# A down projection as seven half-size products per pair of chunks, with its sums on GpSimd and VectorE

## The chip, the cores and the metric

The kernel runs on one core of a Trainium2 chip. The metric is the time of one execution on the device in microseconds (us). Engines are named as in the profile: PE is TensorE, DVE VectorE, ACT ScalarE, POOL GpSimd, SP SyncE, which issues the transfers.

## What is computed

One layer of a decoder for a prompt of 2048 tokens and 32 sample tokens, width 1024. The change concerns the last product of the layer, from the gated activations (2816 wide) to the model width, its residual and the final norm:

```python
h2 = rms_norm(x, p['norm2_w']) * (1.0 + sc2) + sh2
u, val = jnp.split(h2 @ p['w_up'], [D_FF], axis=-1)
u, fbuf_new = causal_dwconv(u, fbuf, p['ffconv_w'], p['ffconv_b'])
x = x + g2 * ((jax.nn.silu(u) * val) @ p['w_down'])
...
y = rms_norm(x, final_w)
```

Inputs and outputs are float32.

## The kernel before

A float32 product is made of float16 parts: each operand is scaled by a power of two and cut into a high part (ScalarE, `ACT.Copy` with a scale) and a low part (VectorE, value times scale minus the high part). `three_passes` (L343) issues three matmuls for one product: high by high, high by low, low by high.

The layer runs in phases, one block of engine programs each; a phase starts when all engines have ended the one before. Inside a phase each engine works through its own program in the order in which it is written, and semaphores order the engines among themselves. The last two phases matter here.

`phase_up` walks over 22 blocks of 128 hidden columns, in three groups of tokens each. It makes its product in seven half-size products as well (`UpWeights`, L2177, whose four weight sums run on GpSimd), writes the activations to DRAM (`act_cols`, one row of 128 hidden columns per block) and keeps their maxima, from which the scale of the next product follows. It also reads `w_down` tile by tile for the weights' maximum. At its end SyncE loads the first two weight pieces and the first part of chunk 0 (`core.first_raw`, `core.first_a`).

`phase_down` (L2694) has the 16 prompt chunks of 128 tokens and one chunk of 32 sample tokens. For a chunk, `product` runs over 22 tiles of K and two halves of the 1024 output columns, 22 x 2 x 3 = 132 matmuls of 128x128 by 128x512, into two PSUM banks; the other two banks serve the next chunk. During chunk 0 the weights arrive in 11 pieces of 2048 columns; ScalarE cuts their high parts (L2819), VectorE their low parts (L2876), and they stay in SBUF as `d_w`. For each chunk ScalarE and VectorE cut the activations in one instruction each (L2812, L2853, 2816 columns). `finish` on VectorE scales the product by the gate (L2863), adds the residual (L2866), waits for ScalarE's sum of squares (L2824), forms the mean (L2868), waits for GpSimd's power of -1/2 (L2908), and multiplies by the final norm (L2870). SyncE stores the rows and loads the next.

## Time and profile before

| | us |
|---|---|
| median of 3 runs | 2749.71 (2747.45 to 2750.07) |
| the profiled execution | 2748.17 |
| its span, first to last instruction | 2746.0 |
| TensorE busy in the span | 2503.5 (91%) |
| VectorE, ScalarE, GpSimd busy | 1675.2, 837.0, 401.8 |
| mean granted clock of TensorE | 0.951 of full speed |

Times inside a profile are counted from the first instruction. A matmul's busy time is longer than its pitch, since matmuls overlap in the engine; the pitch is read from starts. Granted clock 1.00 is 2.4 GHz, 0.50 is 1.2 GHz.

### The profile page before, as it was taken

To read this page: it belongs to the slowest core of one execution; us is meant where nothing else is said; L and a number is where in the kernel's file an instruction comes from. 1 tells how busy PE (TensorE), PEld (TensorE's weight loads), DVE (VectorE), ACT (ScalarE), POOL (GpSimd) and SP (SyncE) were. 2 spreads that over 40 slices of the span, in tenths; PEclk is the share of its full clock that TensorE was granted. 3 is DMA by queue.
4 is the path that set the end of the run, shared out by engine and by line. 5 is a ranking of instruction groups with operands and counts; after the bars stand their busy time and mean duration, and the time that the engine had idled before them with its cause. 6 is when DMAs were issued, how large, how long until landed. Compare 5 with 4: busy or idle time off the path is not lost. (4 is left out here: it accounts for less than half of the span.)

```text
span 2746.0 us, 44479 instructions
## 1 busy us (share of the span) xinstructions
PE 2503.5 (91%) x17421; PEld 1544.9 (56%) x17421; DVE 1675.2 (61%) x3344; ACT 837.0 (30%) x1273; POOL 401.8 (15%) x384
## 2 busy tenths in 40 slices
PE   2699999969998999599969999999999979999998
PEld 0355555558766777455446666666666643444444
DVE  6445565546888787578867777777777765222221
ACT  2324343214434444144422222222223233111110
POOL 0123232300000000012232222122211200000000
PEclk6799999979999999699989999999999999999999
DMA  8335433370232311333311222122221236323221
GB/s 257 104 114 166 147 123 126 117 232 29 85 146 96 144 55 54 101 119 119 118 54 59 72 77 73 62 64 72 77 73 57 70 132 195 110 73 99 82 79 41
DMA packets 194618, 279.69 MB, mean 102 GB/s; under 512 B 16296, under 2 KB 131544, under 8 KB 192332
## 3 DMA queue, kind: packets, MB, share of 16 engines
q1 hardware_dynamic: 194517, 278.34, 31.2%
q8 instruction: 63, 1.03, 0.2%
q14 instruction: 38, 0.31, 0.0%
HBM read 203.02 MB, written 75.29 MB: 101 GB/s over the span
## 5 line engine op out<-in xcount | busy, mean ns | idle before, releaser
L345 PE MATMUL d_po<-d_w,w_heads 128*128 128x512 f16 x704 | 269.1, 382 | 17.2 <-DVE d_w L2876 16.5
L346 PE MATMUL d_po<-d_w,w_heads 128*128 128x512 f16 x704 | 268.9, 382 | 0.0
L347 PE MATMUL d_po<-d_w,w_heads 128*128 128x512 f16 x704 | 268.9, 382 | 0.0
L2379 PE MATMUL py<-h_parts,w_heads 128*128 128x384 f16 (+1 forms) x792 | 246.0, 311 | 18.1 <-DVE u_p L2521 18.1
L2380 PE MATMUL py<-h_parts,w_heads 128*128 128x384 f16 (+1 forms) x792 | 245.8, 310 | 0.0
L2381 PE MATMUL py<-h_parts,w_heads 128*128 128x384 f16 (+1 forms) x792 | 245.8, 310 | 0.0
L345 PE MATMUL prj<-w_heads,h_parts_t 128*128 128x512 f16 x512 | 195.8, 382 | 10.8 <-DVE h_parts_t L962 5.4
L2863 DVE SCALAR_TENSOR_TENSOR d_out<-d_po,d_scale,g_p 128x1024 f32<-128x1024 f32 x16 | 20.5, 1284 | 288.6 <-PE d_po L347 288.5
L346 PE MATMUL prj<-w_heads,h_parts_t 128*128 128x512 f16 x512 | 195.6, 382 | 0.0
L347 PE MATMUL prj<-w_heads,h_parts_t 128*128 128x512 f16 x512 | 195.5, 382 | 0.0
L345 PE MATMUL m_prj<-m_h,w_heads 128*128 128x128 f16 (+1 forms) x1088 | 178.8, 217 | 12.9 <-DMA m_h<-h_parts 11.6
L2379 PE MATMUL px<-h_parts,w_heads 128*128 128x384 f16 (+1 forms) x528 | 164.5, 312 | 17.5 <-PEq L1841 17.5
L346 PE MATMUL m_prj<-m_h,w_heads 128*128 128x128 f16 (+1 forms) x1088 | 178.8, 217 | 0.0
L347 PE MATMUL m_prj<-m_h,w_heads 128*128 128x128 f16 (+1 forms) x1088 | 178.7, 217 | 0.0
L2380 PE MATMUL px<-h_parts,w_heads 128*128 128x384 f16 (+1 forms) x528 | 164.5, 311 | 0.0
L2381 PE MATMUL px<-h_parts,w_heads 128*128 128x384 f16 (+1 forms) x528 | 164.5, 311 | 0.0
L2379 PE MATMUL pz<-h_parts,w_heads 128*128 128x384 f16 (+1 forms) x528 | 163.9, 310 | 0.0
L2380 PE MATMUL pz<-h_parts,w_heads 128*128 128x384 f16 (+1 forms) x528 | 163.9, 310 | 0.0
L2381 PE MATMUL pz<-h_parts,w_heads 128*128 128x384 f16 (+1 forms) x528 | 163.9, 310 | 0.0
L2674 POOL TENSOR_TENSOR u_vz<-u_val,u_cv 128x384 f32<-128x384 f32 (+1 forms) x66 | 60.4, 914 | 621.8 <-DVE u_cv L2561 410.1
L2812 ACT ACTIVATE w_heads<-w_heads,mscale 128x2816 f16<-128x2816 f32 (+1 forms) x16 | 40.5, 2532 | 351.2 <-PE d_po L347 340.3
L345 PEld LDWEIGHTS d_po<-d_w,w_heads 128*128 128x128 f16 x704 | 69.3, 98 | 103.1 <-issue 11.9
(471 smaller groups left out, 5652.0 us busy)
## 6 DMA issues: line engine op xcount, KB each, us to landing
C_new<-in_w_up_dram SPq DMA_DIRECT2D x11, 2048.0 KB, 7.5
w_heads<-in_w_up_dram SPq DMA_DIRECT2D x44, 512.0 KB, 5.8
w_heads<-act_cols SPq DMA_DIRECT2D x15, 1408.0 KB, 7.2
act_cols<-w_heads SPq DMA_DIRECT2D x44, 384.0 KB, 2.3
win_raw<-in_w_in_dram SPq DMA_DIRECT2D x8, 2048.0 KB, 13.9
win_raw<-in_w_ada_dram SPq DMA_DIRECT2D x8, 2048.0 KB
first_a<-in_w_down_dram SPq DMA_DIRECT2D x22, 512.0 KB, 3.7
w_heads<-in_w_down_dram SPq DMA_DIRECT2D x11, 1024.0 KB, 6.3
```

The source lines that it names most:

```text
L345: nc.tensor.matmul(out, left[0], right[0], start=(k == 0), stop=False)
L346: nc.tensor.matmul(out, left[0], right[1], start=False, stop=False)
L347: return nc.tensor.matmul(out, left[1], right[0], start=False, stop=last)
L2379: nc.tensor.matmul(out, left[0], right[0], start=(start and k == 0), stop=False, skip_group_check=True)
L2380: nc.tensor.matmul(out, left[0], right[1], start=False, stop=False, skip_group_check=True)
L2381: last = nc.tensor.matmul(out, left[1], right[0], start=False, stop=(k == KC // 2 - 1), skip_group_check=True)
L2674: last = nc.gpsimd.tensor_tensor(of_half(vz, g, 1), by_pair(ov, g), of_half(cv, g, 1), ALU.mult)
L2812: nc.scalar.activation(ap[buf][:, 0, :, 0:T], a[:, :, 0:T], ACT.Copy, scale=a_scale(c)).then_inc(s["a_hi"], 1)
L2863: last = nc.vector.scalar_tensor_tensor(out=out[0:T], in0=of, scalar=ks[0:T, group(c):group(c) + 1], in1=g[0:T], op0=ALU.mult, op1=ALU.mult)
```

## The change

The 16 prompt chunks become eight pairs. K is split into two halves, the output columns into two halves, and a pair has two chunks of tokens: a two-by-two product of blocks, which Strassen's form (Winograd's variant) makes of seven block products, each with a sum of activation blocks and a sum of weight blocks. The 11 steps over K (`J`) are now the outer loop and the seven products the inner one, each with a PSUM bank of its own; a step is 7 x 3 = 21 matmuls of 512 columns. There are 88 steps, `n` from 0 to 87, pair `i` and K step `j`.

- Weights: for each of the 11 steps GpSimd makes four sums of 128x512 (`sums_w`); ScalarE and VectorE cut three own blocks and four sums (1536 and 2048 columns). 11 transfers of 1 MB, in a ring of three buffers. Step 0's are loaded, summed and cut during the last block of `phase_up`.
- Activations: for each step two transfers of 128 KB into a ring of three; GpSimd makes two sums of 128x128 (`sums_13`), VectorE two more (`sums_24`), and both cuts have 896 columns. Two buffers of parts.
- The seven banks are put together into four output blocks by five VectorE additions that read PSUM and two in SBUF; ScalarE copies two banks out (`keep`). Gate, residual, mean and norm of the two chunks are placed behind steps 0 to 5 of the next pair.
- The sample tokens come after the last pair, as four column groups over 11 steps: 132 matmuls of 512 columns.
- The weights' maximum is found two blocks from the end of `phase_up` (`search`), each tile of `w_down` one block earlier.

The core of the diff (the same waits are on the other engines where they are left out):

```diff
+class DownParts:
...
+    J = FB // 2
+    RAW = (0, 0, 1, 2, 0, 1, 2, 0, 1, 2, 1)
+    SUM = (0, 0, 1, 0, 1, 0, 1, 0, 1, 0, 1)
+    W_OF = (0, 2, 1, 6, 3, 4, 5)
+    A_OF = (1, 2, 6, 0, 3, 4, 5)
...
+    def load_w(self, sp, j):
+        p = self.last_user(self.RAW, j)
+        if p is not None:
+            sp.wait_ge(self.w_lo, 2 * p + 1)
+            sp.wait_ge(self.w_summed, p + 1)
+        sp.dma_start(self.raws[self.RAW[j]].rearrange("p (h n) -> p h n", h=2), self.src_w[j]).then_inc(self.w_in[self.RAW[j]], 16)
...
+    def sums_w(self, pool, j):
+        b, t = self.raw(j), self.tsum(j)
+        b12, b11, b22, b21 = (b[:, q] for q in range(4))
+        p = self.last_user(self.SUM, j)
+        self.w_landed(pool, j)
+        if p is not None:
+            pool.wait_ge(self.w_lo, 2 * p + 2)
+        steps = Steps(pool, self.w_steps, 2 * j)
+        self.nc.gpsimd.tensor_tensor(t[:, 2], b22, b12, ALU.subtract)
+        steps.then(self.nc.gpsimd.tensor_tensor(t[:, 0], b12, b11, ALU.subtract))
+        steps.then(self.nc.gpsimd.tensor_tensor(t[:, 1], b22, t[:, 0], ALU.subtract))
+        self.nc.gpsimd.tensor_tensor(t[:, 3], t[:, 1], b21, ALU.subtract).then_inc(self.w_summed, 1)
+    def w_parts(self, j, i):
+        w = self.slot(j)
...
+    def hi_sums(self, act, j):
+        act.wait_ge(self.w_summed, j + 1)
+        to, of = self.w_parts(j, 0)[1]
+        self.nc.scalar.activation(to, of, ACT.Copy, scale=self.core.mscale[:, 1:2]).then_inc(self.w_hi, 1)
+    def lo_part(self, dve, j, q):
+        dve.wait_ge(self.w_hi, 2 * j + q + 1)
+        (lo, of), (hi, _) = self.w_parts(j, 1)[q], self.w_parts(j, 0)[q]
+        self.nc.vector.scalar_tensor_tensor(out=lo, in0=of, scalar=self.core.mscale[:, 1:2], in1=hi, op0=ALU.mult, op1=ALU.subtract).then_inc(self.w_lo, 1)
+    def a_raw(self, n):
...
+    def load_a(self, sp, n):
+        i, j = divmod(n, self.J)
+        if n > 3:
+            sp.wait_ge(self.a_lo, n - 2)
+        raw = self.a_raw(n)[:, 0:4].rearrange("p (c h) t -> p c h t", c=2)
+        src = self.src_a[j][:, :, 2 * i * P:2 * (i + 1) * P].rearrange("p h (c t) -> c p h t", c=2)
+        sem = self.a_in[3 if n == 0 else n % 3]
+        for c in range(2):
...
+    def sums_13(self, pool, n):
+        a = self.a_raw(n)
+        pool.wait_ge(self.a_in[3 if n == 0 else n % 3], 32 if n == 0 else 32 * ((n + 2) // 3))
+        self.nc.gpsimd.tensor_tensor(a[:, 4], a[:, 0], a[:, 1], ALU.add)
+        self.nc.gpsimd.tensor_tensor(a[:, 6], a[:, 2], a[:, 0], ALU.subtract).then_inc(self.a_half, 1)
+    def sums_24(self, dve, n):
+        a = self.a_raw(n)
+        dve.wait_ge(self.a_half, n + 1)
+        self.nc.vector.tensor_tensor(a[:, 5], a[:, 4], a[:, 2], ALU.subtract).then_inc(self.a_steps, 1)
+        dve.wait_ge(self.a_steps, n + 1)
+        self.nc.vector.tensor_tensor(a[:, 7], a[:, 3], a[:, 5], ALU.subtract).then_inc(self.a_summed, 1)
+    def wait_step(self, eng, n):
+        i, j = divmod(n, self.J)
+        if j == self.J - 1:
+            eng.wait_ge(self.prod, 7 * (i + 1))
+        else:
+            eng.wait_ge(self.k_done, (self.J - 1) * i + j + 1)
+    def cut_a_hi(self, act, n):
+        act.wait_ge(self.a_summed, n + 1)
+        if n > 2:
+            self.wait_step(act, n - 2)
+        self.nc.scalar.activation(self.a_parts(n)[:, 0], self.a_raw(n)[:, 1:8], ACT.Copy, scale=self.a_scale(n // self.J)).then_inc(self.a_hi, 1)
+    def cut_a_lo(self, dve, n):
+        dve.wait_ge(self.a_hi, n + 1)
+        to = self.a_parts(n)
+        self.nc.vector.scalar_tensor_tensor(out=to[:, 1], in0=self.a_raw(n)[:, 1:8], scalar=self.a_scale(n // self.J), in1=to[:, 0],
+                                            op0=ALU.mult, op1=ALU.subtract).then_inc(self.a_lo, 1)
...
-            sp.wait_ge(s["p3"], UG * (FB - 1))
-            sp.dma_start(core.first_raw[0], pairs[0]).then_inc(core.first_in[0], 16)
             sp.wait_ge(up.lo_cut, FB)
-            sp.dma_start(core.first_raw[1], pairs[1]).then_inc(core.first_in[1], 16)
+            dn.load_w(sp, 0)
...
+            dn.load_a(sp, 0)
             body(FB - 1, 1, False)
+            dn.load_w(sp, 1)
...
+                        if last:
+                            act.wait_ge(s["p3"], UG * b)
+                            dn.hi_own(act, 0)
+                        else:
+                            up.cut_hi_sums(act, b + 1, 1 - u)
+                    if g == 2 and last:
+                        dn.hi_sums(act, 0)
...
+            dn.cut_a_hi(act, 0)
...
+                    if g == 0 and search:
+                        dve.wait_ge(s["wd_maxed"], FB)
+                        nc.vector.tensor_reduce(tops.red[:, 0:1], wd_max[:], AX.X, ALU.max).then_inc(tops.found, 1)
...
+                    if g == 2:
+                        if last:
+                            dn.sums_24(dve, 0)
+                            dn.lo_part(dve, 0, 0)
+                        else:
...
+            dn.lo_part(dve, 0, 1)
+            dn.cut_a_lo(dve, 0)
...
                     odd_vz(UG * b + g, g, first and g == 0)
+                    if last and g == 0:
+                        dn.sums_w(pool, 0)
+                        dn.sums_13(pool, 0)
...
+            for n in range(1, J):
+                dn.load_a(sp, n)
+                if n + 1 < J:
+                    dn.load_w(sp, n + 1)
...
+                dn.load_a(sp, n)
+                if j == 5:
+                    save(y_rows[2 * i - 2], 2 * i - 2)
+                    load_x(2 * i - 1)
+                if j == 8:
+                    save(y_rows[2 * i - 1], 2 * i - 1)
+                    load_x(2 * i)
...
+            def step(n):
+                i, j = divmod(n, J)
+                pe.wait_ge(dn.a_lo, n + 1)
+                if i == 0:
+                    pe.wait_ge(dn.w_lo, 2 * j + 2)
+                a, w = dn.a_parts(n), dn.slot(j)
+                for m in ORDER:
+                    if j == 0 and i:
+                        bank_free(m, i - 1)
+                    last = three_passes(nc, pm[:, m], [a[:, x, dn.A_OF[m]] for x in range(2)], [w[:, x, dn.W_OF[m]] for x in range(2)], j, j == J - 1)
+                    if j == J - 1:
+                        last.then_inc(dn.prod, 1)
+                if j < J - 1:
+                    last.then_inc(dn.k_done, 1)
...
+            def keep(i):
+                act.wait_ge(dn.prod, 7 * i + 1)
+                if i:
+                    act.wait_ge(s["saved"], 32 * i)
+                nc.scalar.copy(c11, pm[:, 0]).then_inc(s["kept"], 1)
+                act.wait_ge(dn.prod, 7 * i + 5)
+                nc.scalar.copy(s5, pm[:, 4]).then_inc(s["kept"], 1)
...
+            for j in range(1, J):
+                if j == 9:
+                    act.wait_ge(dn.w_lo, 15)
+                    act.wait_ge(dn.w_summed, 8)
+                if j == 10:
+                    act.wait_ge(dn.w_lo, 20)
+                    dn.wait_step(act, 0)
+                dn.hi_own(act, j)
+                dn.hi_sums(act, j)
+                dn.cut_a_hi(act, j)
+            for n in range(J, N):
+                i, j = divmod(n, J)
+                dn.cut_a_hi(act, n)
+                if j == 0:
+                    keep(i - 1)
+                if j == 2:
+                    square(2 * i - 2)
+                if j == 5:
+                    square(2 * i - 1)
+            act.wait_ge(s["dec_in"], 16)
+            nc.scalar.activation(dec[:, 0, 0:2].rearrange("p h f t -> p h (f t)"), dec_raw, ACT.Copy, scale=core.mscale[:, 3:4]).then_inc(s["dec_hi"], 1)
+            act.wait_ge(s["dec_summed"], 1)
+            nc.scalar.activation(dec[:, 0, 2].rearrange("p f t -> p (f t)"), dec_sum, ACT.Copy, scale=core.mscale[:, 3:4]).then_inc(s["dec_hi"], 1)
+            keep(PAIRS - 1)
...
+            def prepare(n):
+                dn.sums_24(dve, n)
+                dn.cut_a_lo(dve, n)
+            def blocks(i):
+                at = 5 * i
+                dve.wait_ge(dn.prod, 7 * i + 2)
+                dve.wait_ge(s["kept"], 2 * i + 1)
+                nc.vector.tensor_tensor(c12, pm[:, 5], c11, ALU.add).then_inc(s["folded"], 1)
+                dve.wait_ge(dn.prod, 7 * i + 3)
+                dve.wait_ge(s["folded"], at + 1)
+                nc.vector.tensor_tensor(c11, pm[:, 1], c11, ALU.add).then_inc(s["folded"], 1)
+                dve.wait_ge(dn.prod, 7 * i + 4)
+                nc.vector.tensor_tensor(c22, pm[:, 6], c12, ALU.add).then_inc(s["folded"], 1)
+                dve.wait_ge(dn.prod, 7 * i + 6)
+                dve.wait_ge(s["folded"], at + 3)
+                nc.vector.tensor_tensor(c21, c22, pm[:, 3], ALU.subtract).then_inc(s["folded"], 1)
+                dve.wait_ge(dn.prod, 7 * i + 7)
+                nc.vector.tensor_tensor(c12, pm[:, 2], c12, ALU.add).then_inc(s["folded"], 1)
+                dve.wait_ge(s["kept"], 2 * i + 2)
+                dve.wait_ge(s["folded"], at + 5)
+                steps.then(nc.vector.tensor_tensor(c22, c22, s5, ALU.add))
+                steps.then(nc.vector.tensor_tensor(c12, c12, s5, ALU.add))
+            def scale(k, g=None):
+                T, of = rows(k), out_of(k)[0:rows(k)]
+                col = UG - 1 if k == NCH else group(k // 2)
+                steps.then(nc.vector.scalar_tensor_tensor(out=of, in0=of, scalar=ks[0:T, col:col + 1], in1=(g_p if g is None else g)[0:T], op0=ALU.mult, op1=ALU.mult))
+            def residual(k):
+                x = x_of(k)[0:rows(k)]
+                dve.wait_ge(s["x_in" if k < NCH - 1 else f"x_in_{k}"], 16 * k + 16 if k < NCH - 1 else 16)
+                nc.vector.tensor_tensor(x, x, out_of(k)[0:rows(k)], ALU.add).then_inc(s["x2_here"], 1)
+            def mean(k):
+                T = rows(k)
+                dve.wait_ge(s["x_sq"], k + 1)
+                if k:
+                    dve.wait_ge(s["x_rms"], k)
                 nc.vector.tensor_scalar(st[0:T, 1:2], st[0:T, 0:1], 1.0 / D, RMS_EPS, ALU.mult, ALU.add).then_inc(s["x_mean"], 1)
-                dve.wait_ge(s["x_rms"], c + 1)
...
             nc.vector.memset(half[:], -0.5).then_inc(s["half"], 1)
...
+            for j in range(1, J):
+                dn.lo_part(dve, j, 0)
+                dn.lo_part(dve, j, 1)
+                prepare(j)
...
+            for n in range(J, N):
+                i, j = divmod(n, J)
+                prepare(n)
+                if n == J:
+                    dve.wait_ge(s["const"], 32)
+                if j == 0:
+                    blocks(i - 1)
+                if j == 1:
+                    scale(2 * i - 2)
+                    residual(2 * i - 2)
+                if j == 2:
+                    mean(2 * i - 2)
+                    norm(2 * i - 2)
+                if j == 3:
+                    scale(2 * i - 1)
+                if j == 4:
+                    residual(2 * i - 1)
+                if j == 5:
+                    mean(2 * i - 1)
+                    norm(2 * i - 1)
...
+            for k in (NCH - 2, NCH - 1):
+                scale(k)
+                residual(k)
+            for k in (NCH - 2, NCH - 1):
+                mean(k)
+                norm(k)
+            dve.wait_ge(s["dec_here"], 1)
+            steps.then(nc.vector.tensor_tensor(dec_rows[:, 512:D], aux[0:NS, :], dec_rows[:, 512:D], ALU.add))
...
+            for j in range(1, J):
+                dn.sums_w(pool, j)
+                dn.sums_13(pool, j)
+            for n in range(J, N):
+                i, j = divmod(n, J)
+                dn.sums_13(pool, n)
+                if j == 3:
+                    x_rms(2 * i - 2)
+                if j == 6:
+                    x_rms(2 * i - 1)
+            pool.wait_ge(s["dec_in"], 16)
+            nc.gpsimd.tensor_tensor(dec_sum, dec_raw[:, 0], dec_raw[:, 1], ALU.add).then_inc(s["dec_summed"], 1)
```

## Rows read from the trace of the kernel before

**Rows 1.** Windows of the down stage: start and end, us, busy per engine (instructions), granted clock, DMA.

```profile
2250.00:2300.00 50.00, 36.25 (x142) 14.81 (x143) 33.77 (x26) 27.04 (x14) 0.00 (x0) 0.81 0.80 271
2400.00:2457.00 57.00, 57.00 (x266) 25.83 (x264) 14.02 (x10) 7.37 (x6) 1.10 (x2) 1.00 0.30 88
```

**Rows 2.** Chain that ended last: start us, us, what; first and last of 14 equal steps.

```profile
2331.37 0.07 POOL d_stats L2908
...
2701.72 0.07 POOL d_stats L2908
```

**Rows 3.** Timeline of TensorE and VectorE: start us, us, instruction, idle time before it.

```profile
2255.81 0.58 PE L345 MATMUL d_po<-d_w,w_heads 128*128 128x512 f16 x1 [9.26 <-DVE d_w L2876]
...
2327.36 1.28 DVE L2863 SCALAR_TENSOR_TENSOR d_out<-d_po,d_scale,g_p 128x1024 f32<-128x1024 f32 x1 [12.59 <-PE d_po L347]
...
2725.80 0.38 PE L347 MATMUL d_po<-d_w,w_heads 128*128 128x512 f16 x1
...
2741.30 1.27 DVE L2870 SCALAR_TENSOR_TENSOR d_out<-d_x,d_stats,final_w_t 32x1024 f32<-32x1024 f32 x1 [0.65 <-POOL d_stats L2908]
```

**Rows 4.** Groups by line and form, GpSimd, 1150 to 1395: busy us, mean ns.

```profile
L2161 POOL TENSOR_TENSOR o_h_sums<-o_h_full 128x512 f32<-128x512 f32 x8 | 10.2, 1271 | 14.4 <-DVE o_h_full L370 14.4
...
L2161 POOL TENSOR_TENSOR o_h_sums<-o_h_full 128x64 f32<-128x64 f32 x1 | 0.3, 320 | 12.8 <-DVE h_parts L2103 12.8
```

**Rows 5.** Groups by line and form, all engines, down stage.

```profile
L2876 DVE SCALAR_TENSOR_TENSOR d_w<-w_heads,mscale,d_w 128x2048 f16<-128x2048 f32 x11 | 25.6, 2348 | 12.2 <-ACT d_w L2819 12.2
L2819 ACT ACTIVATE d_w<-w_heads,mscale 128x2048 f16<-128x2048 f32 x11 | 21.8, 1996 | 14.5 <-DMA w_heads<-in_w_down_dram 14.5
L2870 DVE SCALAR_TENSOR_TENSOR d_out<-d_x,d_stats,final_w_t 128x1024 f32<-128x1024 f32 x16 | 20.5, 1284 | 10.6 <-POOL d_stats L2908 10.6
...
L2866 DVE TENSOR_TENSOR d_x<-d_x,d_out 128x1024 f32<-128x1024 f32 x16 | 19.6, 1225 | 0.6
L2824 ACT ACTIVATE d_junk<-d_x 128x1024 f16<-128x1024 f32 x16 | 16.7, 1043 | 29.0 <-DVE d_x L2866 29.0
L2908 POOL TENSOR_TENSOR d_stats<-d_stats,d_minus_half 128x1 f32<-128x1 f32 x16 | 8.8, 550 | 476.8 <-DVE d_stats L2868 476.8
...
L2812 ACT ACTIVATE w_heads<-w_heads,mscale 128x704 f16<-128x704 f32 x1 | 0.9, 883 | 24.8 <-PE d_po L347 24.8
```

**Rows 6.** Groups by line and form, VectorE, 1150 to 1395.

```profile
L2097 DVE TENSOR_TENSOR h_parts<-o_h_full,h_parts 128x128 f16<-128x128 f32 x1 | 0.3, 292 | 0.1
```

**Rows 7.** Groups by line and form, VectorE, 1400 to 2245.

```profile
L2228 DVE SCALAR_TENSOR_TENSOR w_heads<-w_heads,up_scale 128x512 f16<-128x512 f32 x21 | 15.5, 738 | 0.0
```

**Rows 8.** Timeline of VectorE, then of GpSimd, 1384 to 1394.

```profile
1385.85 7.22 DVE L2228 SCALAR_TENSOR_TENSOR w_heads<-w_heads,up_scale 128x1024 f16<-128x1024 f32 x3
...
1385.34 1.71 POOL L2162 TENSOR_TENSOR o_h_sums<-o_h_full 128x512 f32<-128x512 f32 x1
1387.13 2.12 POOL L2163 TENSOR_TENSOR o_h_sums<-o_h_full,o_h_sums 128x512 f32<-128x512 f32 x1
1389.33 1.59 POOL L2164 TENSOR_TENSOR o_h_sums<-o_h_full,o_h_sums 128x512 f32<-128x512 f32 x1
```

**Rows 9.** Timeline of VectorE at the end of the up stage.

```profile
2236.42 0.50 DVE L2521 SCALAR_TENSOR_TENSOR u_p<-py,up_kv,u_p 128x272 f32<-128x272 f32 x1 [0.67 <-PE py L2381]
...
2248.44 0.16 DVE L2665 TENSOR_REDUCE tops_red<-u_max 128x1 f32<-128x4 f32 x1
```

**Rows 10.** Two waits of TensorE in the timeline, and the windows behind them.

```profile
2281.57 0.61 PE L345 MATMUL d_po<-d_w,w_heads 128*128 128x512 f16 x1 [4.71 <-DVE d_w L2876]
...
2298.66 0.39 PE L345 MATMUL d_po<-d_w,w_heads 128*128 128x512 f16 x1 [0.67 <-DVE w_heads L2853]
...
2280.00:2284.00 4.00, 2.43 (x6) 0.88 (x7) 3.79 (x2) 3.46 (x2) 0.00 (x0) 0.50 0.74 230
2284.00:2288.00 4.00, 4.00 (x15) 1.63 (x14) 2.43 (x2) 1.80 (x2) 0.00 (x0) 0.74 1.02 407
2296.00:2300.00 4.00, 3.33 (x17) 1.52 (x16) 3.76 (x9) 0.00 (x0) 0.00 (x0) 1.00 0.02 6
```

More of the change, by code:

```diff
@@ L2332, in _, with body @@
             load_wd(0)
-            def body(b, u, more, first=False):
+            load_wd(1)
+            def body(b, u, more, first=False, last=False):
                 if not first:
@@ L2404, in opening, with body @@
                 product(u, g, 6, py[:, x], True).then_inc(s["p6"], 1)
-            def body(b, u, first=False, second=False, last=False):
+            def body(b, u, first=False, search=False, last=False):
                 for g in range(UG):
@@ new lines, in decode @@
+            def decode():
+                pe.wait_ge(s["dec_lo"], 2)
+                for j in range(J):
+                    for a, b in ((0, 0), (0, 1), (1, 0)):
+                        for t, (h, q) in enumerate(((0, 0), (1, 2), (2, 1), (0, 5))):
+                            last = nc.tensor.matmul(aux[NS * t:NS * (t + 1), :], dec[:, a, h, j, :], dn.slot(j)[:, b, q],
+                                                    start=(j == 0 and a == b), stop=(j == J - 1 and a == 1))
+                last.then_inc(s["dec_prod"], 1)
@@ L2798, in _ @@
+            for n in range(N):
+                if n == 2:
+                    tops.turn_rows(pe, 2)
+                if n == 4:
+                    tops.spread_rows(pe, 2)
+                step(n)
+            decode()
         @block.scalar
         def _(act):
[L2800 to L2806 removed]
@@ L2904, in _, with x_rms @@
+            scale(NCH, g_s)
+            residual(NCH)
+            mean(NCH)
+            norm(NCH)
         @block.gpsimd
         def _(pool):
-            def x_rms(c, T):
-                pool.wait_ge(s["x_mean"], c + 1)
+            def x_rms(k):
+                T = rows(k)
+                pool.wait_ge(s["x_mean"], k + 1)
                 nc.gpsimd.tensor_tensor(st[0:T, 2:3], st[0:T, 1:2], half[0:T, 0:1], ALU.pow).then_inc(s["x_rms"], 1)
             pool.wait_ge(s["half"], 1)
-            with pool.Fori(0, NCH) as c:
-                x_rms(c, P)
@@ L2917 @@
+            for k in range(NCH - 2, NCH + 1):
+                x_rms(k)
 _DATA = ["x_prompt", "x_sample", "c_prompt", "c_sample", "state_ret", "state_mlstm_C", "state_mlstm_n", "state_mlstm_m",
```

364 lines of the change are left out of this document (168 added, 196 removed).

## The prediction, made before the result was known

> **What bounds the kernel now.** I read the stage table first, then the chain that ended last, then the groups of instructions, then the timeline of single engines where the change acts.
>
> In the long middle of the down stage TensorE is busy in the whole of its window at granted clock 1.00, while VectorE has 14 us of work in 57, ScalarE 7 and GpSimd 1 [rows 1]. The chain shows the same as a beat: GpSimd's root of a chunk comes every 28.49 us, 13 times over, from 2331.37 to 2701.72 [rows 2]. A chunk is 132 matmuls of 512 columns, so one costs 0.2158 us. Here TensorE sets the time, and a matmul less is 0.2158 us less.
>
> The first two chunks are different. TensorE starts at 2255.81 after 9.26 us of waiting, and VectorE takes the second chunk at 2327.36, so the two took 71.6 us where 57 would do [rows 3]. In 2250 to 2300 TensorE is busy in 36 of 50 us at clock 0.81 [rows 1]: it waits for weights being cut. The last wide matmul starts at 2725.80 [rows 3], and the span ends at 2746.0: a tail of 20.2.
>
> The profiled execution took 2748.17 us, 2.2 more than its span; the median shown is 2749.71. A difference under 0.2% (5.5 us) can't be told from none.
>
> **The change, part by part.**
>
> *The products.* A pair of chunks takes 11 K steps of 7 products of 3 matmuls: 231 in place of 264, 49.86 us in place of 56.98. Over the seven later pairs that is at most 49.8 us less. The shapes are unchanged, and so I take the pitch. One step is 21 matmuls, 4.53 us; whatever hands over a step's operands must keep that beat.
>
> *Pair 0, which cuts the weights.* Each of steps 1 to 10 asks for this, by the nearest rows:
> - GpSimd: four sums of 128x512 at 1.27 and two of 128x128. The add of 64 columns takes 0.32 [rows 4], so by the line through both 128 columns take 0.46. Sum 6.0.
> - ScalarE: cuts of 1536, 2048 and 896 columns. From 2.00 at 2048 and 0.88 at 704 [rows 5]: 1.57, 2.00 and 1.04.
> - VectorE: low parts of 1536, 2048 and 896 columns and two sums of 128x128. From 2.35 at 2048 and 1.28 at 1024 [rows 5]: 1.82, 2.35 and 1.15; the sums 0.29 each [rows 6]. Sum 5.9.
>
> None alone is over 6.0, but they stand in a row. VectorE's program has the two activation sums behind both weight parts, ScalarE's cut of the activations waits for these sums, and ScalarE's next weight cut is queued behind it. One turn is therefore 1.57 + 2.00 + 2.35 + 0.6 + 1.04, plus some 0.04 a handover: 7.8 us a step. That is the lower bound.
>
> The upper bound comes from GpSimd and VectorE together. In the trace they don't run side by side when both read two tensors from SBUF. From 1385.85 VectorE's three low parts, of 1024, 512 and 2048 columns, take 7.22 us; alone these cost 1.28, 0.74 and 2.35, 4.4 together [rows 5, 7, 8]. In the same stretch GpSimd's sums of 1.27 take 1.71, 2.12 and 1.59 [rows 8]. They alternate: from 1385.34 to 1393.07 7.73 us pass over 8.2 us of work (4.4 and three sums), so a change of hands gives back about 0.15. All five VectorE instructions and all six GpSimd instructions of a step have two SBUF inputs. Together they are 11.9 us; ten changes of hands take off 1.5. I take 10.4 us a step, since the three measured low parts are the same operation on the same types; 7.8 and 11.9 stay as ends.
>
> The Trainium skill, page "SBUF — State Buffer", section "SBUF: two separate sides", calls this port pair an exclusive lock, held for the whole instruction, against which the other engine fully blocks. By that rule, with nothing given back, a step costs 11.9 and the time would be 15 us longer than my sum; the rows give the 0.15 back, and I go by them.
>
> Step 1 has no step ahead of it to overlap with: its weight sums (5.1) and ScalarE's cut of them (2.0) precede the turn, so I add 7. The last step's matmuls add 4.7. Pair 0: 7 + 10 x 10.4 + 4.7 = 115.7 us, against 71.6 for the two chunks before. The weight transfers (1 MB a step, 11 in all, as before) hide under this. TensorE's clock will fall in the gaps, as after the gap of 4.71 at 2281.57 [rows 10], but a step at half clock is 9.1, still under 10.4.
>
> *Pairs 1 to 7.* What is queued on VectorE decides. At a pair's first step it recombines the seven banks of the pair before, and its last additions can only start when the last product is done. Behind them in its queue stand the sums for the pair's second step. From the end of the last product: 0.2 (the matmul's tail), three additions of 128x512 at 0.69 (by 1.225 at 1024 and 0.29 at 128 [rows 5, 6]), two sums of 0.29, two GpSimd sums of 0.46 that slip in on the port, ScalarE 1.04, VectorE 1.15, and 0.4 of handovers: 6.3 us, and TensorE has 4.53 us of work in hand. Stall 1.8. At the next step scale (1.28) and residual (1.23) stand ahead of 0.6 + 1.1 + 1.2: with handovers 5.5, stall 1.0. Then mean, GpSimd's root (0.55) and norm (1.28) [rows 5] ahead of the same: 5.4, stall 0.9. At j = 3 and 4 there are 4.2 and 4.1, no stall; at j = 5 mean, root and norm again, 5.1 against 4.53: 0.5 with some slack gained. Sum 4.2 a pair, 54.1 us in place of 57.0. Bounds: 0 if the queue keeps up, 6 if each of these instructions loses another GpSimd sum. Seven pairs: 378.4 us. Activation loads (256 KB a step, three buffers) have three steps of time and cost nothing.
>
> *The end of the up stage.* VectorE's last instruction there starts at 2248.44 [rows 9]. Ahead of it now stand two sums and the low part of 1536 columns (2.4 us; 0.67 of idle time before 2236.42 [rows 9] takes some up: +1.7), behind it the low parts of 2048 and 896 columns (3.6). It ends near 2254, the next phase opens there, and TensorE needs no wait then: first matmul at 2254.8, 1.0 earlier than now. The earlier search for the weights' maximum adds some 2 us of small VectorE work two blocks from the end, where VectorE waits for TensorE; I take 0.3 of it.
>
> *The tail.* After the last matmul: three additions (2.4), scale and residual for two chunks (5.1), mean, root and norm twice with a square between (4.3), two additions for the decode rows (1.5), then scale, residual, square, mean, root, norm (5.9) and the store as now, 3.4 from VectorE's end (2741.30 and 1.27 [rows 3], span 2746.0). That is 22.6, against 20.2. The decode product, 132 matmuls, hides under the first half.
>
> *Sum.* 2254.8 + 115.7 + 378.4 + 22.6 = 2771.5; plus 2.2: **2774 us**, 0.9% slower. What seven products save over pairs 1 to 7 (20 us after stalls) is less than what pair 0 loses (44).
>
> **Rivals.**
> - *The port doesn't bind in pair 0* (faster). GpSimd's sums fall in time where VectorE waits for ScalarE, and the turn stays 7.8. It decides at one point: forecast and median are 24 us apart, so at 8.0 us a step the change breaks even. For it: VectorE idles 1.9 us of the 7.8. Against it: the six sums need 6.0. Pair 0 is then 12 + 9 x 7.8 + 4.7 = 87, the stalls lose the GpSimd slots (0.9 a pair): 2739 us.
> - *The port gives nothing back.* 11.9 a step and 6 of stall: 2801 us.
> - *TensorE's clock falls at the pair boundaries.* Seven banks are filled in turn with short pauses. Against it: the gap of 0.67 at 2298.66 left the clock at 1.00; for it: the one of 4.71 brought 0.50, and 0.74 in the four us behind, some 4 us at half clock and 2 us lost [rows 10]. Once a pair: 2789 us. The Trainium skill, "TensorE: Matmul & The Clock Gate", section "A second HAM failure mode: psum-queue depth-cycling", describes such a fall when PSUM banks are cycled at 512 columns; no row of this stage shows it, and where TensorE is full it stays at 1.00 [rows 1].
> - *Pairs without stalls.* Slack built up in j = 6 to 10 covers the boundary and all seven-eighths arrives: 2744 us.
>
> **How the numbers follow.** Forecast 0.62 (own range 2760 to 2788), port free 0.13, port without give-back 0.10, clock 0.07, no stalls 0.08. The range must leave out at most 2 in 10: from 2744, which drops the port-free case, to 2796, which drops half of the port without give-back: 0.18 outside. Slower by over 0.2%: 0.75, from the forecast without its low edge, the port and the clock; within: 0.10; faster: 0.15, the port-free case and the edge of the last.
>
> **What would show it.** Right: pair 0 takes 105 to 125 us with TensorE under half busy, VectorE's 2048-column low parts run over 3 us there, GpSimd's 128x512 sums over 1.6; later pairs take 53 to 56 with gaps at their second, third and fourth steps; tail near 22.6. Wrong: a turn under 8.5 us in pair 0, VectorE's low parts at 2.35, or a granted clock below 1 after 2400.

## The result, and the profile after

The changed kernel takes **2768.0 us** (median of 4 runs, 2765.78 to 2769.63) against 2749.0 before, measured beside it: a ratio of 1.0069, 95% interval 1.0052 to 1.0086. It is slower by 0.7%. The prediction was 2774. The profiled execution took 2766.77 us with a span of 2765.0.

Windows of the changed kernel show the three parts of the down stage: pair 0, pairs 1 to 7, and what follows the last wide matmul. The columns are those of [rows 1].

```profile
2256.50:2371.30 114.80, 67.61 (x235) 26.11 (x236) 93.70 (x65) 46.43 (x33) 101.08 (x66) 0.80 0.39 127
...
2371.30:2742.40 371.10, 353.14 (x1618) 155.85 (x1616) 229.50 (x338) 102.50 (x120) 101.93 (x164) 1.00 0.32 95
2742.40:2765.00 22.60, 7.58 (x134) 3.44 (x132) 15.24 (x18) 5.18 (x9) 1.63 (x3) 0.74 0.17 59
```

GpSimd had nothing to do in the down stage's first 50 us before [rows 1]; now it is busy for 101 of 115 us in pair 0, and TensorE for only 68, at a granted clock of 0.80. From 2371.3 on TensorE is busy for 353 of 371 us at a clock of 1.00, that is 2.4 GHz: 53.0 us a pair, where the same two chunks took 57.0.

Against the sum of the prediction (profiled execution, us):

| term | predicted | measured |
|---|---|---|
| first wide matmul | 2254.8 | 2256.55 |
| pair 0, to the first matmul of step 11 | 115.7 | 114.7 |
| pairs 1 to 7 | 378.4 (54.06 each) | 371.1 (53.0 each) |
| behind the last wide matmul | 22.6 | 22.6 |
| span | 2771.5 | 2765.0 |

One step of pair 0, in the timeline of the changed kernel, VectorE first and then GpSimd (start us, us, instruction, idle time before it):

```profile
2326.50 2.19 DVE L2377 SCALAR_TENSOR_TENSOR w_heads<-d_a,mscale,w_heads 128x896 f16<-128x896 f32 x1 [1.11 <-ACT w_heads L2372]
2328.61 6.10 DVE L2322 SCALAR_TENSOR_TENSOR d_w<-w_heads,mscale,d_w 128x1536 f16<-128x1536 f32 x2
2334.64 0.54 DVE L2357 TENSOR_TENSOR d_a<-d_a 128x128 f32<-128x128 f32 x1
2335.20 0.43 DVE L2359 TENSOR_TENSOR d_a<-d_a 128x128 f32<-128x128 f32 x1
...
2326.48 1.26 POOL L2301 TENSOR_TENSOR d_work<-d_work 128x512 f32<-128x512 f32 x1
2327.82 2.01 POOL L2302 TENSOR_TENSOR d_work<-d_work 128x512 f32<-128x512 f32 x1
2329.90 2.66 POOL L2303 TENSOR_TENSOR d_work<-d_work 128x512 f32<-128x512 f32 x1
2332.53 2.49 POOL L2350 TENSOR_TENSOR d_a<-d_a 128x128 f32<-128x128 f32 x1
2334.99 0.50 POOL L2351 TENSOR_TENSOR d_a<-d_a 128x128 f32<-128x128 f32 x1
```

Read it as pairs of neighbours. VectorE's two weight parts, 1.82 and 2.35 when nothing disturbs them, take 6.10 together; GpSimd's activation sum of 128x128, 0.45 alone, takes 2.49, because it sits out a VectorE instruction first. On TensorE steps 5 to 9 start between 10.0 and 10.2 us apart. From step 1 to step 10 the mean is 10.4, as predicted, but with two unequal steps in it (see below, on why the prediction was right).

### The profile page after: what moved, and what is told of

It is laid out like the page before. It is cut to its first block and busy times, and to the rows that moved or that the text cites. A ratio compares the mean times of both kernels' runs of the same rounds, so it can differ in the third digit from the quotient of the medians.

```text
span 2765.0 us, 44410 instructions
## 1 busy us (share of the span) xinstructions
PE 2467.0 (89%) x17028; PEld 1515.4 (55%) x17028; DVE 1877.4 (68%) x3669; ACT 910.1 (33%) x1371; POOL 602.1 (22%) x605
## 5 line engine op out<-in xcount | busy, mean ns | idle before, releaser
L345 PE MATMUL d_pm<-d_w,w_heads 128*128 128x512 f16 x392 | 153.5, 392 | 56.4 <-DVE w_heads L2377 56.2
L2377 DVE SCALAR_TENSOR_TENSOR w_heads<-d_a,mscale,w_heads 128x896 f16<-128x896 f32 x87 | 107.7, 1238 | 136.1 <-ACT w_heads L2372 136.1
L2372 ACT ACTIVATE w_heads<-d_a,mscale 128x896 f16<-128x896 f32 x87 | 90.6, 1042 | 313.4 <-DVE d_a L2359 221.1
L345 PE MATMUL m_prj<-m_h,w_heads 128*128 128x128 f16 (+1 forms) x1088 | 179.6, 218 | 11.6 <-DMA m_h<-h_parts 10.3
L346 PE MATMUL d_pm<-d_w,w_heads 128*128 128x512 f16 x392 | 152.7, 390 | 0.0
L347 PE MATMUL d_pm<-d_w,w_heads 128*128 128x512 f16 x392 | 152.3, 388 | 0.0
L2711 DVE SCALAR_TENSOR_TENSOR u_cv<-w_heads,u_conv,u_cv 128x768 f32<-128x768 f32 x132 | 122.3, 927 | 2.4
```

Source lines behind the costliest of these rows:

```text
L345: nc.tensor.matmul(out, left[0], right[0], start=(k == 0), stop=False)
L346: nc.tensor.matmul(out, left[0], right[1], start=False, stop=False)
L347: return nc.tensor.matmul(out, left[1], right[0], start=False, stop=last)
L2372: self.nc.scalar.activation(self.a_parts(n)[:, 0], self.a_raw(n)[:, 1:8], ACT.Copy, scale=self.a_scale(n // self.J)).then_inc(self.a_hi, 1)
L2377: self.nc.vector.scalar_tensor_tensor(out=to[:, 1], in0=self.a_raw(n)[:, 1:8], scalar=self.a_scale(n // self.J), in1=to[:, 0], op0=ALU.mul ...
L2711: ins = nc.vector.scalar_tensor_tensor(out=cv[:, 0:n], in0=ub[:, t:t + n], scalar=cw[:, u, j:j + 1], in1=cv[:, 0:n], op0=ALU.mult, op1=ALU ...
```

## The experiments

Two questions: what makes a step of pair 0 last 10.4 us, and what makes TensorE wait at three steps of each later pair. The theory is the prediction's: GpSimd's sums and VectorE's two-input operations exclude each other, and the activation sums stand too far back in VectorE's queue. The rivals are the order of the queues (for pair 0) and banks freed late (for the later pairs). Nine kernels; all edits are made to the changed kernel. In the table, pair 0 runs from the first wide matmul to step 11, which starts 4.53 us (21 matmuls) after step 10; times are of the profiled execution, but for the last column, the median of the runs (a single run for e1, e2 and e7 to e9).

| kernel | first wide matmul | pair 0 | pairs 1 to 7, each | runs |
|---|---|---|---|---|
| changed kernel | 2256.55 | 114.7 | 53.0 | 2768.0 |
| e1: weight sums left out | 2256.68 | 86.9 | 53.1 | 2739.6 |
| e2: four fills instead | 2256.74 | 83.4 | 53.2 | 2736.8 |
| e7: ten fills instead | 2255.14 | 89.5 | 53.1 | 2740.6 |
| e8: four copies instead | 2257.23 | 90.0 | 53.2 | 2744.0 |
| e9: ten copies instead | 2258.19 | 125.8 | 53.3 | 2781.2 |
| e3: weight sums on VectorE | 2262.68 | 110.2 | 53.0 | 2765.9 |
| e4: activation sums a step ahead | 2256.16 | 113.0 | 50.4 | 2749.7 |
| e6: all activation sums on GpSimd | 2259.12 | 118.0 | 50.2 | 2751.3 |
| e5: e3, e4 and the search | 2254.32 | 97.8 | 50.5 | 2730.1 |

**e1: the weight sums left out.**

```diff
+        if j not in (0, 2):
+            self.nc.gpsimd.tensor_tensor(t[:, 3, 0:1], b22[:, 0:1], b12[:, 0:1], ALU.subtract).then_inc(self.w_summed, 1)
+            return
...
```

> GpSimd's weight sums are left out at every step but j = 0 and 2 (one column is still computed, and ScalarE and VectorE cut the older sums), so the output is not the reference's; every other instruction and every wait stays. Theory (GpSimd's sums and VectorE's two-input operations exclude each other, and that sets the 10.4 us of a step in pair 0): a step falls to the chain of VectorE and ScalarE alone, 7.8 to 8.2 us, VectorE's 2048-column low parts fall from 2.85 to about 2.35, pair 0 takes about 87 us in place of 114.7, the kernel about 2740. Rival (the order of the instructions in VectorE's and ScalarE's queues, or the weight transfers, set the 10.4): pair 0 stays within 5 us of 114.7, the kernel at 2763 to 2770.

The sums of step 2 stay, and step 2 comes 12.4 us after step 1. Pair 0 took 86.9 us, 27.8 less; the run 2739.6, 28 less. A step of VectorE in this kernel's timeline:

```profile
2309.08 4.25 DVE L2325 SCALAR_TENSOR_TENSOR d_w<-w_heads,mscale,d_w 128x1536 f16<-128x1536 f32 x2 [0.31 <-ACT d_w L2315]
2313.24 0.28 DVE L2360 TENSOR_TENSOR d_a<-d_a 128x128 f32<-128x128 f32 x1
2313.56 0.29 DVE L2362 TENSOR_TENSOR d_a<-d_a 128x128 f32<-128x128 f32 x1
2314.96 1.15 DVE L2380 SCALAR_TENSOR_TENSOR w_heads<-d_a,mscale,w_heads 128x896 f16<-128x896 f32 x1 [1.11 <-ACT w_heads L2375]
```

Same order, same waits, and the two weight parts take 4.25 where they took 6.10. The step is 7.35: the queues' order alone doesn't hold it at 10.4. It doesn't yet say whether GpSimd disturbs VectorE or only delivers late.

**e2 and e7: fills in place of the sums.** Four fills a step in e2; ten, one after the other, in e7, so that GpSimd is busy for as long as with its sums.

```diff
+        if j:
+            for q in range(4):
+                last = self.nc.gpsimd.memset(t[:, q], 0.25)
+            last.then_inc(self.w_summed, 1)
+            return
```

> GpSimd's four weight sums of each step j from 1 to 10 are replaced by four fills of the same four 128x512 tiles with a constant (the sums are left out, so the output is not the reference's): GpSimd is still busy and still writes as much, but reads nothing from SBUF. Theory (what excludes VectorE is GpSimd reading two tensors from SBUF): VectorE's low parts run at about 2.35 us at 2048 columns and pair 0 takes 83 to 92 us, the kernel 2736 to 2746. First rival (GpSimd busy in any way holds VectorE off, writes too): the low parts stay over 2.7 us beside the fills and pair 0 stays over 100 us. Second rival (GpSimd is only late with its results): as the theory if a fill takes under 1.2 us, with no step longer than GpSimd's own four fills and two sums.

> GpSimd's four weight sums of a step are replaced by ten fills of 128x512 one after the other (no sums, so the output is not the reference's): by the 0.525 us of a fill some 5.3 to 6 us of GpSimd work a step, as much as the four sums of 1.27, but without a read of SBUF. Theory (GpSimd's reads exclude VectorE, its being busy does not): VectorE's low parts stay at 2.34 at 2048 columns and pair 0 takes 85 to 97 us. Rival (the pair is long because GpSimd is busy for so long and delivers late): pair 0 at 105 us or more.

Both came out as the theory said: 83.4 and 89.5 us. Groups by line and form of e7, from 2256.5 to 2344 (busy us, mean ns, idle time before):

```profile
L2302 POOL MEMSET d_work<- 128x512 f32 x45 | 23.6, 524 | 4.7 <-DMA d_work<-in_w_down_dram 2.4
L2302 POOL MEMSET w_heads<- 128x512 f32 x43 | 22.5, 524 | 2.2
...
L2328 DVE SCALAR_TENSOR_TENSOR d_w<-w_heads,mscale,d_w 128x2048 f16<-128x2048 f32 x4 | 9.4, 2345 | 4.6 <-ACT d_w L2323 4.6
```

GpSimd writes for 5.2 us a step, and VectorE's 2048 columns take 2.345 us, as in the kernel before, 2.348 [rows 5]. A busy GpSimd costs VectorE's parts nothing as long as it only writes.

**e8 and e9: copies in place of the sums.** Four in e8, ten in e9: one tensor read where a sum reads two. The edit is that of the fills with `tensor_copy(t[:, q], b[:, q])`.

> GpSimd's four weight sums of a step are replaced by four copies of 128x512 from the landed weights into the same tiles (no sums, so the output is not the reference's): each reads one tensor from SBUF where a sum reads two. If a read of any kind takes the port from VectorE's two-input operations: the low parts of 2048 columns run at 2.6 us or more and pair 0 lies between 95 and 115 us. If only GpSimd operations with two inputs exclude VectorE: 2.35 and 83 to 92 us, as with the fills.

> GpSimd's four weight sums of a step are replaced by ten copies of 128x512 (no sums, so the output is not the reference's): by the 0.585 us of a copy that meets nothing, 5.9 us a step, as long as the fills of the earlier run (10 x 0.525) and the sums (4 x 1.27), with one tensor read where a sum reads two. If a GpSimd operation that reads one tensor from SBUF excludes VectorE's low parts as a sum does: 5.9 of VectorE, 5.9 of copies and 0.9 of activation sums less the hand-backs, a step of 10.5 to 12.5 us and pair 0 at 112 to 135 us. If only two-input operations exclude each other: as with the ten fills, pair 0 at 85 to 95 us and the 2048-column low parts at 2.35.

e8 came out between its two forecasts: pair 0 took 90.0, near the fills, but the 2048-column parts took 2.40 to 2.54 us (means of four groups by form), more than with fills. Its copies are short, and GpSimd has time to lose (its timeline, GpSimd):

```profile
2276.18 6.92 POOL L2301 COPY d_work<-w_heads 128x512 f32<-128x512 f32 x4
...
2300.54 2.34 POOL L2301 COPY w_heads<-w_heads 128x512 f32<-128x512 f32 x4 [4.99 <-DVE d_w L2327]
```

Three of the ten groups of copies fall into VectorE's pauses and take 2.34, 0.585 a copy, as the second row. Four meet VectorE's parts and take 6.1 to 6.9, as the first; the delay falls on GpSimd, and VectorE loses little. With ten copies, e9, GpSimd has no time to spare. Its timeline, VectorE and then GpSimd:

```profile
2339.00 2.80 DVE L2328 SCALAR_TENSOR_TENSOR d_w<-w_heads,mscale,d_w 128x2048 f16<-128x2048 f32 x1 [3.22 <-ACT d_w L2323]
...
2337.70 10.26 POOL L2302 COPY d_work<-d_work 128x512 f32<-128x512 f32 x9
```

Nine copies that take 5.3 alone take 10.26, and a step 11.70, inside the 10.5 to 12.5 expected if a single read excludes VectorE. Here most of the loss falls on GpSimd, and VectorE then waits 3.22 for ScalarE, which waits for GpSimd. Same number and size of operations as the fills of e7, and 36 us more in pair 0. Undisturbed, ten copies and two sums would be 6.8 us of GpSimd, less than the 7.4 to 7.7 of most steps of e7. It is the read from SBUF that excludes the other engine.

That agrees with the Trainium skill, page "SBUF — State Buffer", section "SBUF: two separate sides", which lets a VectorE operation with two SBUF inputs compete only with a GpSimd operation that reads SBUF. By its rule that the loser is held for the whole instruction a step of the changed kernel would, by estimate, cost 11.9 (5.9 of VectorE and 6.0 of GpSimd); from step 5 to step 9 the steps take 10.0 to 10.2. That doesn't show the rule wrong: the records of one engine's instructions overlap too (in e1 the two weight parts end at 2313.33, and the sum behind them starts at 2313.24), so a sum of recorded times counts some time twice.

**e3: the weight sums on VectorE.**

```diff
-        self.nc.gpsimd.tensor_tensor(t[:, 2], b22, b12, ALU.subtract)
+        on = on or self.nc.gpsimd
+        on.tensor_tensor(t[:, 2], b22, b12, ALU.subtract)
...
                 dn.lo_part(dve, j, 1)
+                if j + 1 < J:
+                    dn.sums_w(dve, j + 1, nc.vector)
                 prepare(j)
...
-                dn.sums_w(pool, j)
                 dn.sums_13(pool, j)
```

> The four weight sums of steps 1 to 10 move from GpSimd to VectorE, one step ahead of their use; GpSimd keeps the two activation sums. Theory (the two engines exclude each other, so the sums cost their GpSimd time of 1.27 each wherever VectorE has work): on VectorE a sum costs about 0.69, a step is VectorE's own 5.9 + 4 x 0.69 = 8.7 us and at most 9.2 with the two activation sums slipping in, pair 0 takes 98 to 104 us, the kernel 2751 to 2757. Rival (GpSimd's sums lie beside VectorE's work and only the chain between ScalarE and VectorE counts): 2.8 us are added to VectorE's chain, a step is over 10.4 and the kernel at 2768 or slower.

A miss: pair 0 took 110.2, not 98 to 104, and the runs 2765.9 (ratio to before 1.0052, interval 1.0036 to 1.0069). This execution also came to the down stage 6 us late, with nothing edited ahead of it, so only its stages are compared. One step of VectorE in its timeline:

```profile
2297.18 1.82 DVE L2323 SCALAR_TENSOR_TENSOR d_w<-w_heads,mscale,d_w 128x1536 f16<-128x1536 f32 x1 [0.32 <-ACT d_w L2313]
2299.07 2.35 DVE L2323 SCALAR_TENSOR_TENSOR d_w<-d_work,mscale,d_w 128x2048 f16<-128x2048 f32 x1
2301.34 0.94 DVE L2301 TENSOR_TENSOR w_heads<-d_work 128x512 f32<-128x512 f32 x1
2302.21 0.94 DVE L2302 TENSOR_TENSOR w_heads<-d_work 128x512 f32<-128x512 f32 x1
...
2306.23 1.15 DVE L2378 SCALAR_TENSOR_TENSOR w_heads<-d_a,mscale,w_heads 128x896 f16<-128x896 f32 x1 [1.11 <-ACT w_heads L2373]
```

The parts are undisturbed (1.82, 2.35), so the port is nearly free. But my 8.7 counted VectorE's work alone. The row has 9.15 of work (two of the four sums at 0.94 beside GpSimd's 128x128 sums) and 1.43 of idle time: 1.11 while ScalarE cuts the activations, 0.32 while it cuts the next weights. The starts lie 10.52 apart. Without the port as the limit, the turn between VectorE and ScalarE is the limit, at nearly the same length. That is close to the rival's number, and the turn is what the rival named; its other half, that GpSimd's sums lie beside VectorE's work at no cost, is refuted by e1, e7 and e9.

**e4: the activation sums a step ahead.**

```diff
             def prepare(n):
-                dn.sums_24(dve, n)
                 dn.cut_a_lo(dve, n)
+                if n + 1 < N:
+                    dn.sums_24(dve, n + 1)
...
+            dn.sums_24(dve, 1)
```

> VectorE's two activation sums are issued one step ahead: behind the low part of step n stand the sums for step n + 1, and only then the additions, scale, residual, mean and norm of the pair before. Nothing else changes. Theory (the stalls of pairs 1 to 7, 2.8 us a pair, come from the sums being queued behind that work, so that ScalarE's cut and VectorE's low part start late; pair 0 is set by the exclusion of GpSimd and VectorE, whatever the order): pairs 1 to 7 fall from 53.0 to 49.9 to 51 us each, pair 0 stays at 108 to 117, the kernel 2746 to 2757. Rival A (the stalls come from the banks being freed late): pairs 1 to 7 stay at 53, kernel 2765 to 2770. Rival B (pair 0 is set by the turn VectorE - ScalarE, not by the port): pair 0 falls to 75 to 95 and the kernel below 2740.

Both halves came out: pairs 1 to 7 take 50.4 each, and pair 0, 113.0, hardly moves. The runs, 2749.7, equal the kernel before (0.9999, interval 0.9989 to 1.0008). In later pairs, ScalarE's cut (L2372) waited 161.6 us in all for VectorE's sums in the changed kernel, and 92.4 for TensorE. The waits of e4, 2374 to 2722 (us in total, times, longest):

```profile
ACT w_heads L2372 <- PE d_pm L347: 194.5, 68, 3.5
...
ACT w_heads L2372 <- DVE d_a L2359: 29.9, 7, 6.3
...
PEld d_pm L345 <- DVE w_heads L2377: 5.4, 7, 2.0
```

Now the cut waits for TensorE to give a buffer back, as it should. Pair 0 in the same kernel's timeline, VectorE's whole step:

```profile
2335.57 1.33 DVE L2377 SCALAR_TENSOR_TENSOR w_heads<-d_a,mscale,w_heads 128x896 f16<-128x896 f32 x1
2337.26 1.33 DVE L2357 TENSOR_TENSOR d_a<-d_a 128x128 f32<-128x128 f32 x1 [0.35 <-POOL d_a L2351]
2338.63 1.24 DVE L2359 TENSOR_TENSOR d_a<-d_a 128x128 f32<-128x128 f32 x1
2339.78 6.17 DVE L2322 SCALAR_TENSOR_TENSOR w_heads<-d_work,mscale,w_heads 128x1536 f16<-128x1536 f32 x2
```

VectorE no longer waits 1.11 us for ScalarE, and yet the step is 10.30: two sums of 0.29 take 1.33 and 1.24. Time taken out of the queue goes to the port. With the order changed the port holds the step at 10.3 (here), with GpSimd's sums gone the order holds it at 10.5 (e3).

**e6: all four activation sums on GpSimd**, the split undone.

```diff
+        if n:
+            pool.wait_ge(self.a_half, n + 1)
+            self.nc.gpsimd.tensor_tensor(a[:, 5], a[:, 4], a[:, 2], ALU.subtract).then_inc(self.a_steps, 1)
+            pool.wait_ge(self.a_steps, n + 1)
+            self.nc.gpsimd.tensor_tensor(a[:, 7], a[:, 3], a[:, 5], ALU.subtract).then_inc(self.a_summed, 1)
...
             def prepare(n):
-                dn.sums_24(dve, n)
```

> The split of the activation sums is undone: GpSimd computes all four sums of every chunk pair's step, none stands in VectorE's queue. Theory: in pairs 1 to 7 nothing but the activation's transfer is ahead of GpSimd's sums, so that the stalls vanish as with the sums a step ahead (50.4 us a pair in place of 53.0); in pair 0 two sums of 0.29 on VectorE become two of 0.46 on GpSimd, both on the same port: 0.2 to 0.5 us a step more, 117 to 120. Kernel 2750 to 2756. Rival A (the sums' place in VectorE's queue is not what stalls the pairs): pairs stay at 53, the kernel at 2768 to 2774. Rival B (GpSimd's longer chain of four sums is late in pair 0 by more than the port takes): pair 0 over 125.

As expected: 50.2 a later pair, 118.0 in pair 0, runs 2751.3 (1.0001, interval 0.9992 to 1.001). Out of VectorE's queue or earlier in it, the sums no longer stall the pairs; on the port they cost more on GpSimd than on VectorE. Windows of e6, pair 0 and the later pairs:

```profile
2259.10:2377.10 118.00, 72.21 (x235) 27.14 (x236) 82.74 (x41) 46.20 (x33) 113.37 (x88) 0.80 0.37 121
2377.10:2728.70 351.60, 349.32 (x1618) 157.71 (x1616) 186.40 (x187) 103.32 (x120) 208.58 (x315) 1.00 0.34 101
```

GpSimd is busy for 113 of 118 us in pair 0. TensorE is busy for 349 of 352 behind it.

**e5: both limits lifted at once.** The edits of e3 and e4, and in the up stage TensorE's transpose for the early maximum moves behind the last product of its group:

```diff
-                    if search and g == 0:
-                        pe.wait_ge(s["frow_here"], b - 1)
-                        pe.wait_ge(s["us_here"], b)
-                        tops.turn_rows(pe, 0)
...
+                    if search and g == 0:
+                        pe.wait_ge(s["frow_here"], b - 1)
+                        pe.wait_ge(s["us_here"], b)
+                        tops.turn_rows(pe, 0)
```

> Three edits of the earlier runs and of the trace together: VectorE's activation sums a step ahead, the weight sums of steps 1 to 10 on VectorE, and TensorE's transpose of the column maxima, in the up stage, moved from ahead of the second to behind the last product. Theory: with the sums ahead VectorE no longer idles 1.11 us for ScalarE's cut, so that a step of pair 0 is VectorE's own work: low parts 1.82 + 2.35 + 1.15, weight sums 0.94 + 0.94 + 0.69 + 0.69, activation sums 0.57, together 9.1 and with handovers 9.3; pair 0 is 12 + 10 x 9.3 = 105 (114.7 before the edits), pairs 1 to 7 are 50.4 each as with the sums ahead alone, TensorE's wait of 2.63 is gone: 2735 to 2742. Rival: the turn through ScalarE still counts (a step over 10), then the kernel is as with the sums ahead alone less the 2.6: 2745 to 2749.

2730.1 us (5 runs, 2729.25 to 2733.72), below the range expected: 0.9928 of the kernel before, interval 0.9915 to 0.9942, and 38 us under the changed kernel. Pair 0 takes 97.8, the later pairs 50.5. Windows of e5: pair 0, the stretch from the start of its step 1 to that of step 10, the later pairs:

```profile
2254.30:2352.20 97.90, 64.51 (x235) 25.39 (x236) 90.40 (x105) 46.17 (x33) 30.78 (x24) 0.84 0.45 145
2270.05:2347.63 77.58, 53.04 (x193) 20.78 (x193) 76.41 (x88) 37.17 (x26) 26.72 (x18) 0.85 0.36 112
2352.20:2705.50 353.30, 350.25 (x1617) 157.32 (x1616) 226.92 (x337) 103.31 (x120) 103.68 (x165) 1.00 0.34 101
```

VectorE is busy for 76.4 of 77.6 us: nothing but its own work is left in a step. Most steps take 8.75 us, where I had 9.3 with the handovers, and the last of these, with no weight sums in it, 5.8; the mean is 8.6. e3 alone took 4.5 us off pair 0, e4 alone 1.7, the two together 16.9. TensorE's first wide matmul comes 2.2 us earlier than in the changed kernel. Executions differ by as much there, but the block of `phase_up` with the search can be compared by itself. From one of VectorE's copies into `u_in_s` to the next it takes 38.3 us in the kernel before, 41.6 in the changed kernel and in six of the others, 43.3 in e3 and e6, and 38.8 in e5: the edit gives back 2.8. In e5's timeline the transpose of the maxima waits for nothing:

```profile
2172.53 0.27 PE L196 MATMUL pt<-identity,tops_red 128*4 128x128 f32 x1
```

## Why the prediction was right

**Pair 0 (115.7 predicted, 114.7 measured): mechanism right, the size in part by luck.** e1, e2, e7 and e9 show the mechanism: without GpSimd's reads the step is, from step 3 on, 7.35 to 7.9 (8.5 to 11.0 where VectorE also computes powers of two), with reads of another kind it is mostly 11.7.

Two terms that my sum left out nearly cancel in the mean of 10.4. From step 4 to step 5 it takes 15.1, since VectorE's eight small operations for powers of two last 5.9 us there (shown in the last section); the last step, beside which GpSimd has no weight sums left, takes 7.7. The other seven intervals average 10.1.

The hand-back came out by luck as well. In the stretch from which I took the 0.15 [rows 8] I overlooked one VectorE instruction, held at its start, and shared what is left over, 8.2 less 7.73, among three changes of hands; with that instruction there are six. The timeline of the kernel before has it just ahead of the lines shown:

```profile
1384.72 1.21 DVE L2097 TENSOR_TENSOR h_parts<-o_h_full,h_parts 128x512 f16<-128x512 f32 x1 [0.69 <-ACT h_parts L2002]
```

With 0.7 us for it, by a VectorE sum of 128x512 (0.69), 7.73 us pass over 8.9, and a change gives back 0.19. The two slips offset each other: in the changed kernel 10.2 us pass over 11.9, with ten changes, 0.16 to 0.17 each.

The lower bound was too high. The turn is the one I wrote down, but e1 runs it in 7.35, not 7.8: in its timeline an instruction starts up to 0.1 us before the one ahead of it on its engine ends (ScalarE's cuts start at 2306.54, 2307.49 and 2308.95 and last 1.04, 1.56 and 1.99), where I added time for handovers. For the rival "the port doesn't bind" my turn gave 87 in all, and e1, with the port taken away, measured 86.9; that agreement too is partly luck, since e1 reaches step 1 after 9.2 us, not 12, and loses the difference at step 2, whose sums it keeps.

Two of the signs I named did not come out: VectorE's 2048-column low parts average 2.9 us in pair 0, not over 3, and TensorE is busy for 59% of it, not under half, since its matmuls take longer at the lower clock (0.63 us each at 0.50, 0.38 at 1.00).

**Pairs 1 to 7 (54.06 each predicted, 53.0 measured): mechanism right, stalls too long.** I had 1.8 + 1.0 + 0.9 + 0.5 = 4.2 a pair; measured are about 1.5 + 0.7 + 0.7 and no fourth, 2.9 (3.1 in the mean of the seven pairs). (Matmuls start 0.22 apart; where the row of TensorE gives a wait of 0.54, starts lie 0.92 apart, 0.70 lost.) One boundary in the changed kernel's timeline, TensorE, then VectorE, then GpSimd:

```profile
2431.00 0.39 PE L345 MATMUL d_pm<-d_w,w_heads 128*128 128x512 f16 x1 [1.33 <-DVE w_heads L2377]
2436.25 0.39 PE L345 MATMUL d_pm<-d_w,w_heads 128*128 128x512 f16 x1 [0.54 <-DVE w_heads L2377]
...
2425.83 0.68 DVE L3058 TENSOR_TENSOR d_work<-d_pm,d_work 128x512 f32<-128x512 f32 x1
...
2427.34 0.69 DVE L3062 TENSOR_TENSOR d_work<-d_work 128x512 f32<-128x512 f32 x1
2428.07 0.29 DVE L2357 TENSOR_TENSOR d_a<-d_a 128x128 f32<-128x128 f32 x1
2428.39 0.29 DVE L2359 TENSOR_TENSOR d_a<-d_a 128x128 f32<-128x128 f32 x1
2429.79 1.15 DVE L2377 SCALAR_TENSOR_TENSOR w_heads<-d_a,mscale,w_heads 128x896 f16<-128x896 f32 x1 [1.11 <-ACT w_heads L2372]
...
2425.86 0.46 POOL L2350 TENSOR_TENSOR d_a<-d_a 128x128 f32<-128x128 f32 x1 [3.68 <-DMA d_a<-act_cols]
```

The chain is as written: additions, the two sums, ScalarE, the low part, TensorE. In its 6.3 us two terms were wrong, with opposite signs. And the additions end 3.0 us after the last product, at 2428.0, not 2.3, since VectorE only came to the first of the seven at 2423.05. At the second and third step VectorE's chain takes 5.24, not 5.5 and 5.4; the fourth stall is covered by what steps 3 and 4 gain. Together 1.06 a pair, 7.3 us in seven: the whole of the miss in the span (6.5), and a little more. e4 and e6 show that it is the queue and not the banks: 50.4 and 50.2 a pair, against 49.86 without stalls.

**The end of the up stage (2254.8 predicted, 2256.55 measured): one term mis-sized.** For the early search of the maximum I took 0.3 us. The timeline of the changed kernel, TensorE and then VectorE:

```profile
2170.88 0.27 PE L196 MATMUL pt<-identity,tops_red 128*4 128x128 f32 x1 [2.63 <-DVE tops_red L2765]
...
2170.56 0.17 DVE L2765 TENSOR_REDUCE tops_red<-u_wd_max 128x1 f32<-128x22 f32 x1
```

I looked at VectorE, which has time to spare there. But the transpose of its result is queued on TensorE ahead of the second product, and TensorE, which has none, waits 2.63 us for it. It is a wait put in front of other work on the engine that sets the end. The block with the search grows by 3.3 us (38.3 to 41.6, as counted under e5), 3.0 more than I took; the rest of the stage's end came out 1.2 us shorter than predicted.

**The tail (22.6 and 22.6)** and **the clock** came out. In the later pairs the clock stays at 1.00 through waits of 0.54 to 2.17 us, so the rival of a clock that falls at pair boundaries is wrong here. The fall with PSUM banks cycled at 512 columns of which the Trainium skill tells, page "TensorE: Matmul & The Clock Gate", section "A second HAM failure mode: psum-queue depth-cycling", does not appear with seven banks.

In all: the seven-eighths arrives almost whole in seven pairs of eight (57.0 to 53.0, and 50.4 with the sums ahead), and 43 us go back in pair 0, the only one in which weights are cut.

## What to carry to other kernels

Before work moves to an idle engine, ask what it reads: where a row shows two engines taking turns, the sum to compare is that of both engines' work, and an operation belongs on the engine where it is shortest (0.69 to 0.94 on VectorE against 1.27 on GpSimd), however busy that engine is. When two limits lie close together (10.3 us of port, 10.5 us of turn), each edit alone gains little; lift both before giving one up. In a queue written by hand, issue what other engines wait for ahead of what only the store waits for, and let no engine that sets the end wait for a result that isn't needed yet.
